# A trunk of gated DeltaNet and RWKV-7: more products behind the norms, the RWKV lora products first, convolution taps in PSUM

## The reference

```python
for i in range(2):
    h = h + 0.5 * rms_norm(swiglu(rms_norm(h, ng[0]), ffn_w_in, ffn_w_out), ng[1])
    u = rms_norm(h, ng[2])
    out = gdn_mixer(u, ...) if i == 0 else rwkv_mixer(u, ...)
    h = h + rms_norm(out, ng[3])
    h = h + 0.5 * rms_norm(swiglu(rms_norm(h, ng[4]), ...), ng[5])

def gdn_mixer(x, ...):
    qkv, z, b, a = split(x @ w_in)                  # 3072, 1024, 8, 8 columns
    qkv = silu(causal_dwconv(concat(conv_buf, qkv), conv_w))      # 4 taps
    q, k = l2_normalize(q), l2_normalize(k)         # per head
    o = rms_norm(chunk_gated_delta(q, k, v, g, beta, s0)) * silu(z)
    return o @ w_out

def rwkv_mixer(x, shift_prev, ...):
    x_prev = concat(shift_prev, x[:, :-1])
    xs = x[:, :, None] + (x_prev - x)[:, :, None] * lerp          # six mixes
    r, k, v = (xs[i] @ w_rkv[i] for i in 0, 1, 2)
    logw = f(w0 + tanh(xw @ w1) @ w2); a = sigmoid(a0 + (xa @ a1) @ a2)
    g = sigmoid(xg @ g1) @ g2
    kk = l2_normalize(heads(k * k_k))
    y = rwkv7_recurrence(r, decay, k, v, -kk, kk * a, s0)
    return (group_norm(y) + bonus) * g @ w_o
```

## Time and profile before

| | |
|---|---|
| median of 3 runs | 3081.12 us (3074.25 to 3081.9) |
| the profiled execution | 3077.95 us |
| its span, first to last instruction | 3076.2 us |
| mean granted TensorE clock | 0.934 of full speed |
| busy: PE, DVE, POOL, ACT | 2716.0, 1217.1, 1070.2, 859.6 us |
| instructions on PE, DVE, ACT, POOL | 26353, 1425, 1165, 506 |
| DMA | 202.15 MB, mean 66 GB/s |

### The profile page before, as it was taken

How to read it: one execution, slowest core, us unless ns; L and a number is a source line. 1 busy time by engine, 2 the same in 40 slices (tenths; PEclk the granted TensorE clock), 3 DMA queues, 4 the chain that set the end, 5 groups by cost and what they waited for, 6 DMA issues and landing times.

```text
span 3076.2 us, 60534 instructions
## 1 busy us (share of the span) xinstructions
PE 2716.0 (88%) x26353; PEld 2569.8 (84%) x26353; DVE 1217.1 (40%) x1425; ACT 859.6 (28%) x1165; POOL 1070.2 (35%) x506
## 2 busy tenths in 40 slices
PE   6999989977988799999899998677649888899997
PEld 6999989855874799999899997677438876899996
DVE  2333138815535443321433322332484455433312
ACT  3222232222321332222322222233413322422221
POOL 2444423323411334444244432232173321244432
PEclk9999999998986899999999998888759999999998
DMA  3223212210002222232122221121100011122321
GB/s 129 88 82 104 85 54 82 75 58 2 2 22 96 69 69 89 88 99 80 55 89 89 92 94 54 56 69 35 35 1 4 4 45 64 63 87 84 101 85 48
DMA packets 52570, 202.15 MB, mean 66 GB/s; under 512 B 6208, under 2 KB 6336, under 8 KB 52160
## 3 DMA queue, kind: packets, MB, share of 16 engines
q1 hardware_dynamic: 52416, 199.82, 19.4%
HBM read 190.12 MB, written 9.67 MB: 65 GB/s over the span
## 4 chain that ended last, share of the span: by engine, by line
PE 41%; issue 34%; POOL 11%; DVE 10%; ACT 1%; DMA 1%; DVEq 0%; POOLq 0%; SPq 0%; ACTq 0%
POOL wlo L271 10%; PE ps L301 10%; PE ps L299 10%; PE ps L300 10%; DVE cb L815 3%; PE ps L2022 1%; PE ps L2030 1%; PE ps L566 1%; PE ps L1973 1%; DVE sFM L2200 1%; PE ps L571 1%; PE ps L2081 1%; PE ps L1446 1%; DVE tb L1722 1%; PE ps L1978 1%
## 5 line engine op out<-in xcount | busy, mean ns | idle before, releaser
L271 POOL TENSOR_TENSOR wlo<-raw,whi 128x1024 fp32r<-128x1024 f32 (+1 forms) x316 | 834.5, 2643 | 1530.3 <-ACT whi L263 1530.3
L299 PE MATMUL ps<-xh,whi 128*128 128x272 f32 x3776 | 1107.7, 293 | 61.4 <-POOL wlo L271 40.5
L301 PE MATMUL ps<-xh,wlo 128*128 128x272 f32 x3776 | 1106.0, 293 | 0.0
L300 PE MATMUL ps<-xl,whi 128*128 128x272 f32 x3776 | 1098.9, 291 | 0.0
L299 PEld LDWEIGHTS ps<-xh,whi 128*128 128x128 f32 x3776 | 723.3, 192 | 77.5 <-POOL wlo L271 38.7
L300 PEld LDWEIGHTS ps<-xl,whi 128*128 128x128 f32 x3776 | 725.3, 192 | 0.0
L301 PEld LDWEIGHTS ps<-xh,wlo 128*128 128x128 f32 x3776 | 722.8, 191 | 0.0
L263 ACT ACTIVATE whi<-raw 128x1024 fp32r<-128x1024 f32 (+1 forms) x316 | 354.3, 1124 | 1277.6 <-PE ps L301 1230.6
L301 PE MATMUL ps<-mh,wlo 128*128 128x272 f32 x1408 | 406.3, 289 | 0.0
L300 PE MATMUL ps<-ml,whi 128*128 128x272 f32 x1408 | 405.5, 288 | 0.0
L299 PE MATMUL ps<-mh,whi 128*128 128x272 f32 x1408 | 405.2, 288 | 0.0
(11 more groups left out here) (397 smaller groups left out, 2919.0 us busy)
## 6 DMA issues: line engine op xcount, KB each, us to landing
raw<-w SPq DMA_DIRECT2D x252, 512.0 KB, 3.5
raw<-w SPq DMA_DIRECT2D x64, 704.0 KB, 4.0
h<-xT SPq DMA_DIRECT2D x1, 2176.0 KB, 11.1
yT<-h SPq DMA_DIRECT2D x1, 2176.0 KB, 6.6
Sst<-state_gdn SPq DMA_DIRECT2D x4, 512.0 KB, 3.5
SG<-state_gdn SPq DMA_DIRECT2D x4, 512.0 KB, 3.5
gdn_s_s<-gG SPq DMA_DIRECT2D x4, 512.0 KB, 2.6
gdn_s_s<-gT SPq DMA_DIRECT2D x4, 512.0 KB, 2.6
```

The source lines that it names most:

```text
L271: pool.tensor_tensor(wlo[two][:, 0:kt * P], raw[slot][:, 0:kt * P], whi[two][:, 0:kt * P].bitcast(F32), ALU.subtract).then_inc(w_lo, 1)
L299: pe.matmul(o, wh, hi[:, r, :], start=(start and k == 0), stop=False)
L300: pe.matmul(o, wh, lo[:, r, :], start=False, stop=False)
L301: mm = pe.matmul(o, wl, hi[:, r, :], start=False, stop=(stop and k == kt - 1))
```

## The change

- **Behind each pre-norm** (the four FFN inputs, the GDN input and now the lora units) PE runs units 0 and 1 and one half of unit 2 tile by tile, then unit 2's other half, the spread and unit 3. Units 0 and 1 have buffers of their own (`EARLY`), and units 0 to 2 are split during the last unit of the product before; unit 3 right behind the post-norm's root. A tiny square root in the same place (`warm`) loads ACT's table. The sums and spreads go to free columns of other banks. In post_norm_dve the low half of the tile before stands ahead of the update of h.
- **GDN input.** From unit 4 on the taps 0 to 2 accumulate in PSUM banks 4 to 7, and only two pairs of banks take units. ACT's split of unit 5 stands behind the second silu. The sums of squares follow one z unit later; the last pair comes after the b and a unit.
- **RWKV.** The lora products (w1|a1 and g1, each once plain and once scaled by the lerp, four units) go directly behind the norm, on the normed x; the token shift is applied to their results (lora_dve). Two rows of 24 matmuls with 8 columns take the carried shift state. DVE scales two raw units in place. The shift of x is done in two halves between the mixes of r; tanh, copy and sigmoid of the lora results stand on ACT between r and k; the squares and sums of k stand beside the units of v.

The core of the diff:

```diff
-    ("r", NM, NM), ("k", NM, NM), ("v", NM, NM), ("lora", 3, NM), ("wo", NM, NM),
+    ("lora", 4, NM), ("r", NM, NM), ("k", NM, NM), ("v", NM, NM), ("wo", NM, NM),
...
+        def early_hi(act, name, j):
+            n = BASE[name] + j
+            act.wait_ge(raw_in[n % 4], 16 * (n // 4 + 1))
+            if name == "lora" and j > 1:
+                act.wait_ge(R["lw_up"], past(R["lw_up"], j - 1))
+            free = 2 * (BASE[name] - (j < 3))
+            if free > 0:
+                act.wait_ge(acc, free)
+            dst = EARLY[name][0][j] if j < 2 else whi[n % 2]
+            act.activation(dst[:, 0:NM * P], raw[n % 4][:, 0:NM * P], ACT.Copy).then_inc(w_hi, 1)
...
+        def behind_norm_mm(pe, name, q):
+            behind_norm_tiles(pe, name, q)
+            behind_norm_half(pe, name)
+            spread_norm_pe(pe, q)
+            unit_mm(pe, name, 0, 3, pair(3), xh, xl)
+
+        def behind_norm_tiles(pe, name, q):
+
+            base = BASE[name]
+            bufs = [(EARLY[name][0][j], EARLY[name][1][j]) for j in range(2)] + [(whi[base % 2], wlo[base % 2])]
+            for k in range(NM):
+                pe.wait_ge(x_lo, 8 * SETS[name] + k + 1)
+                for j in range(3):
+                    if k == 0:
+                        pe.wait_ge(w_lo, base + j + 1)
+                    if j == 1:
+                        square_sum_pe(pe, q, k)
+                    first_products(pe, j, k, *bufs[j], halves=(0, 1) if j < 2 else (0,))
+            if q:
+                pe.wait_ge(h_upd, 8 * (q // 2))
+
+        def behind_norm_half(pe, name):
+            two = BASE[name] % 2
+            for k in range(NM):
+                first_products(pe, 2, k, whi[two], wlo[two], halves=(1,))
...
-                dve.tensor_tensor(tb[3][:, :, :], y[:, 2 * m:2 * m + 2, :], pair(3), ALU.mult).then_inc(h_tmp, 1)
+                dve.tensor_tensor(tb[3][:, :, :], y[:, 2 * m:2 * m + 2, :], post_rows(), ALU.mult).then_inc(h_tmp, 1)
+                if sett is not None and m:
+                    pre_norm_low(dve, q + 1, sett, m - 1)
                 dve.wait_ge(h_tmp, base + m + 1)
                 dve.scalar_tensor_tensor(h[:, 2 * m:2 * m + 2, :], tb[3][:, :, :], step,
                                          h[:, 2 * m:2 * m + 2, :], ALU.mult, ALU.add).then_inc(h_upd, 1)
-                if sett is not None and m:
-                    pre_norm_low(dve, q + 1, sett, m - 1)
...
                     if last and j >= 2:
                         split_hi(act, f"ffn{f}_out", 0, j - 2)
+                    elif first:
+                        if j == 0:
+                            split_hi(act, name, 0, 4)
+                            norm_copy_act(act, FFN_NORM[f])
+                        elif j == 3:
+                            split_hi(act, name, 0, 5)
                     else:
                         split_hi(act, name, 4 * i, j + 2)
...
+                    if last and j == 3:
+                        act.activation(warm[:, q // 2:q // 2 + 1], eps[:, 0:1], ACT.Sqrt)
+                        if then is not None:
+                            for jj in range(2 if then == "lora" else 3):
+                                early_hi(act, then, jj)
...
-                    split_hi(act, "gdn_in", 4 * i, j + 2)
                     if first and j == 0:
+                        split_hi(act, "gdn_in", 0, 4)
                         norm_copy_act(act, 2)
-                    else:
-                        silu_out(idx - 1, 1 - e)
+                        continue
+                    if not first:
+                        split_hi(act, "gdn_in", 4 * i, j + 2)
+                    elif j == 3:
+                        split_hi(act, "gdn_in", 0, 5)
+                    silu_out(idx - 1, 1 - e)
...
-                    n = EXT - 3
-                    dve.tensor_scalar(cb[e][:, 0:n], ext[e][:, 0:n], col(0), None, ALU.mult).then_inc(S["cv"], 1)
+                    part = two_rows(cb[e], 0) if first else taps_bank(e)
+                    dve.tensor_scalar(part, two_rows(ext[e], 0), col(0), None, ALU.mult).then_inc(S["cv"], 1)
                     for tap in range(1, 4):
                         dve.wait_ge(S["cv"], 5 * idx + 1 + tap)
-                        dve.scalar_tensor_tensor(cb[e][:, 0:n], ext[e][:, tap:tap + n], col(tap), cb[e][:, 0:n],
+                        dve.scalar_tensor_tensor(two_rows(cb[e], 0) if tap == 3 else part, two_rows(ext[e], tap), col(tap), part,
                                                  ALU.mult, ALU.add).then_inc(S["cv"], 1)
...
-            first_units_mm(pe, "gdn_in", q=2)
-            third_fourth_mm(pe, "gdn_in", 2)
-            with pe.Fori(1, NQKV // 4) as i:
+            behind_norm_mm(pe, "gdn_in", 2)
+            for j in range(4):
+                pe.wait_ge(S["ext_ready"], (1, 2, 5, 6)[j])
+                unit_mm(pe, "gdn_in", 4, j, pair(j % 2), xh, xl)
+            with pe.Fori(2, NQKV // 4) as i:
                 for j in range(4):
-                    pe.wait_ge(S["ext_ready"], 4 * i + j - 3)
-                    unit_mm(pe, "gdn_in", i * 4, j, pair(j), xh, xl)
+                    pe.wait_ge(S["ext_ready"], 4 * i + j - 1)
+                    unit_mm(pe, "gdn_in", i * 4, j, pair(j % 2), xh, xl)
 
             for m in range(HG):
-                if m < 3:
-                    pe.wait_ge(S["ext_ready"], NQKV - 3 + m)
+                if m < 2:
+                    pe.wait_ge(S["ext_ready"], NQKV - 1 + m)
+                elif m == 2:
+                    pe.wait_ge(S["cv"], 5 * (NQKV - 1))
                 else:
                     pe.wait_ge(S["z_scaled"], m - 2)
                 unit_mm(pe, "gdn_in", NQKV + m - m % 4, m % 4, pair(m % 3), xh, xl)
-                if m == 0:
-                    pe.wait_ge(S["ext_ready"], NQKV)
-                for t in (2 * m, 2 * m + 1):
-                    pe.wait_ge(S["l2_sq"], t + 1)
-                    sum_rows(pe, pair(3), one_col[:, 15 - t:31 - t], tb[t % 2], t == 0, t == 15).then_inc(S["l2_mm"], 1)
+                if m == 1:
+                    pe.wait_ge(S["cv"], 5 * NQKV)
+                if m > 0:
+                    l2_sums(pe, (2 * m - 2, 2 * m - 1))
...
+        def key_square_act(act, m):
+            if m == 0:
+                act.wait_ge(x_lo, 8 * SETS["wo"])
+            if m - 1 > 0:
+                act.wait_ge(R["kq_mm"], past(R["kq_mm"], m - 1))
+            act.activation(tb[m % 2][:, :, :], wh(k_, m), ACT.Square, scale=v(V_KK + m)).then_inc(R["kq_sq"], 1)
+
+        def key_sum_pe(pe, m):
+            pe.wait_ge(R["kq_sq"], past(R["kq_sq"], m + 1))
+            sum_rows(pe, pair(3), two_cols[:, 14 - 2 * m:30 - 2 * m], tb[m % 2], m == 0, m == NM - 1).then_inc(R["kq_mm"], 1)
...
+        def lora_scale_dve(dve):
+            for j, parts in ((2, ((3, slice(0, 64)), (4, slice(64, P)))), (3, ((5, slice(0, P)),))):
+                n = BASE["lora"] + j
+                dve.wait_ge(raw_in[n % 4], 16 * (n // 4 + 1))
+                w = raw[n % 4][:, 0:NM * P].rearrange("p (m c) -> p m c", c=P)
+                for i, c in parts:
+                    lerp = vec[:, V_LERP + i * NM:V_LERP + (i + 1) * NM].unsqueeze(2).broadcast_to([P, NM, c.stop - c.start])
+                    mul = dve.tensor_tensor(w[:, :, c], w[:, :, c], lerp, ALU.mult)
+                mul.then_inc(R["lw_up"], 1)
+            dve.wait_ge(R["sh_hi"], past(R["sh_hi"], 1))
+            dve.tensor_tensor(sh_l[:, :, :], shin[:, :, :], sh_h[:, :, :].bitcast(F32), ALU.subtract).then_inc(R["sh_lo"], 1)
...
+        def lora_out_act(act):
+            act.wait_ge(R["lora_up"], past(R["lora_up"], 12))
+            act.activation(lt1[0:64, :, :], LT[0][0:64, :, :], ACT.Tanh)
+            act.activation(lt1[64:P, :, :], LT[0][64:P, :, :], ACT.Copy).then_inc(R["lora_cp"], 1)
+            act.activation(lg[:, :, :], LT[1][:, :, :], ACT.Sigmoid).then_inc(R["lora_cp"], 1)
+            act.wait_ge(R["lora_cp"], past(R["lora_cp"], 2))
...
+            base = BASE["lora"]
+
+            def carried(j):
+                n = base + j
+                pe.wait_ge(w_lo, n + 1)
+                o = ps[:, 6, HALF + NB * (j - 2):HALF + NB * (j - 1)]
+                for k in range(NM):
+                    wh_, wl_ = (t[n % 2][:, k * P:(k + 1) * P] for t in (whi, wlo))
+                    pe.matmul(o, wh_, sh_h[:, k, :], start=(k == 0), stop=False)
+                    pe.matmul(o, wh_, sh_l[:, k, :], start=False, stop=False)
+                    pe.matmul(o, wl_, sh_h[:, k, :], start=False, stop=(k == NM - 1))
+            behind_norm_tiles(pe, "lora", 8)
+            pe.wait_ge(R["sh_lo"], past(R["sh_lo"], 1))
+            carried(2)
+            behind_norm_half(pe, "lora")
+            carried(3)
+            pe.wait_ge(R["lora_raw"], past(R["lora_raw"], 2))
+            spread_norm_pe(pe, 8)
+            unit_mm(pe, "lora", 0, 3, pair(3), xh, xl)
...
+                dve.tensor_tensor(prev[:, :, :], prev[:, :, :], rs[:, :, :], ALU.mult).then_inc(up, 1)
```

(18 more changed lines are left out.)

274 lines of the change are left out of this document (158 added, 116 removed).

## The result

The kernel after takes 2985.32 us (median of four runs, 2982.70 to 2988.54); the kernel before, beside it, 3078.62 (four runs). The ratio is 0.9698, with a 95% interval of 0.9680 to 0.9716: 93.3 us less. The forecast was 2986.

A forecast was written before the change was run, and what follows sets the result against it. TensorE (PE), busy for 88% of the span, was taken as the bound, with gains where it stands idle. Terms sum to -94.5 against 3077.95: 2983.5, forecast 2986 since the median is 3.2 above that execution; range 2960 to 3014.

The forecast's parts named there:

- The three sites: Norms in front of the three inner FFN inputs: -4.8, -5.1 and -4.7 us, bounds -2 and -7 each.
- the start: Kernel's start, up to the first FFN's end: only the product's part of the norm gain, -2.5 us (0 to -3).
- just over DVE's pace of about 2.25: Tiles behind the norms: 15 matmuls and sums take 2.4 us at full clock, just over DVE's 2.25.
- The reciprocal behind `sh_l`: RWKV head: reciprocal behind DVE's wait for ACT's copy of the shift state, some 2.4 us before the first lora product.
- 4.8 for 2 x 24 tiny matmuls ... between them: RWKV head, before r: 48 tiny matmuls at 0.1 us each, taken between bounds of nothing and 7.9.
- r itself: RWKV: the shift's second half between the mixes of r adds 4 us (0 to +8).
- r to k: RWKV: ACT's tanh, copy and sigmoid with two table loads ahead of the next weights add 4.4 us.
- v's eight sums: RWKV, in v: eight sums of 1.0 us, of which about 5 us show.
- The first rival: Convolution: DVE stays the bound, as PSUM-writing instructions are held up or take longer; 2999 us, chance 0.13.
- the second: RWKV gives back half, its new head being one long chain through DVE and ACT; +20, 3006 us, chance 0.15.
- the third: Convolution: DVE's PSUM accumulation makes the kernel slower than before, from about 2.4 us per instruction; 3097 at 2.6, chance 0.02.
- the fourth: Norm parts do little, longer tiles running at the low clock; -1 at three sites and start, 2999 us, chance 0.10.

The follow-up runs named there:

- The late splits: Kernel after, but units 0 to 3 behind each of five norms are all split behind the post-norm's root: 3004.56 us, 0.9757.
- the other trace: The kernel after run once more, unchanged, on one chip with three edits: 2987.09 us, 0.9708; span 2979.6. Also called the second trace.
- the old RWKV stage's run: Kernel after, but the RWKV mixer up to the norm of k as before, lora last on mixed x: 3029.49 us, 0.9836.
- the sums of k's norm: Kernel after, but squares of k beside k's units and all eight sums in PE's gap between k and v: 2976.84 us, 0.9677.

## Why the prediction held, step by step

**Norms: right in size, wrong in one reason.** The three sites gave -5.8, -4.8 and -4.7 for -4.8, -5.1 and -4.7; the start -2.4 for -2.5. The late splits show that the early ones are worth 3.8 a norm, through POOL's absence beside `h` and `xl`. The step "just over DVE's pace of about 2.25" failed: PE is the bound of the tiles, before (2.08 us each) as after (2.45), and no worth of the half unit abreast is seen (2986.03 without it). The last norm gave 0.1 for 0.4.

**Convolution: right.** Forecast: four instructions of about 0.85, a DVE unit near 5.2, PE the bound at 6.04. Measured: 0.81, and PE units 6.04 apart. The first z unit ends 13.1 us earlier (13.2 forecast): at 600.5, one unit before the first sums at 606.51, and 172.0 us behind the first FFN instead of 185.1. The timeline of after: the first DVE unit with taps in PSUM, from one unit's first scaling (L875) to the next, and the copy of a later unit beside POOL's split:

```profile
484.62 0.43 DVE L875 TENSOR_TENSOR ext<-ps,rs 128x272 f32<-128x272 f32 x1
...
489.62 0.17 DVE L894 COPY cnew<-ext 128x3 f32 x1
489.77 0.44 DVE L875 TENSOR_TENSOR ext<-ps,rs 128x272 f32<-128x272 f32 x1
...
578.86 1.12 DVE L894 COPY cnew<-ext 128x3 f32 x1
...
577.56 2.40 POOL L300 TENSOR_TENSOR wlo<-raw,whi 128x1024 fp32r<-128x1024 f32 x1 [3.65 <-ACT whi L275]
```

That unit takes 5.15 us (489.77 - 484.62). Later each takes 6.04, because the copy of three columns is held until POOL's split ends (577.56 + 2.40 = 579.96; the copy ends at 579.98). This wait costs nothing: POOL is paced by ACT, ACT by PE, and the slack of 0.9 is DVE's to lose. In before POOL's split stood beside the three multiply-adds and cost 2.24.

The Trainium skill (VectorE: DVE Perf Modes, section "Why PSUM operands drop a tier") says that an operand in PSUM caps fp32 at the slowest mode. The multiply agrees: 516 ns for 568 columns into SBUF, 812 into PSUM. By that alone the change adds 0.3 a unit; the lock it escapes was worth more.

**z part: right.** Forecast -23 between the first z unit and the spread; it takes 69.7 us (670.14 - 600.5) instead of 92.7, and the whole GDN input gave -36.1 for -36. The sums in their own unit cost 14.6, by the trace in PE's wait for ACT's squares (15.5).

**RWKV: right in sum, with four terms off.** From FFN2's last product to r's first it is 58.4 us (57.0 in the other trace), 54.6 forecast. Two terms failed. The reciprocal behind `sh_l` cost 3.3, priced at 2.4. And "4.8 for 2 x 24 tiny matmuls ... between them" was right for themselves (5.3) but left out the clock that they lose in this trace: half unit 2 took 4.60 at 0.63 where 3.0 was forecast, and the spread and unit 3 8.7 where 7.1 was. In the second trace these took 3.1 and 7.2. r itself took 3.9 more for 4, and r to k was 4.7 longer for 4.4: right. PE at the end of v in after:

```profile
2101.32 4.17 PE L627 MATMUL ps<-tb,mf 128*16 128x272 f32 x16
2106.50 2.18 PE L1981 MATMUL ps<-lt,wa 64*128 64x272 f32 x16 [1.02 <-ACT tb L2003]
...
2118.04 2.10 PE L1794 MATMUL ps<-tb,halves 128*128 128x272 f32 x8 [1.39 <-ACT RB L2007]
```

Here the sums are mis-sized in the other direction: v's eight sums all show (four of 1.09 inside v, four in the 4.17 behind it), +8.5 for +5; from the last of them to the norm of k it is 12.5 us (2118.04 - 2105.49), where 17 was forecast and 24.6 stood: -12.1 for -7.7. Of the 3.3 priced for the root and two table loads PE waited only 1.02 us, since the root's load ran beside the last sums and the sigmoid's beside the first decay products. The terms' errors, up to 4.4 each way, partly cancel: -38.3 for -41 in these traces; by its medians the old stage costs 44.2.

**The rest.** Sum of the terms: -94.5 forecast, -89.7 between the two spans, -93.3 between the medians. That the median hits 2986 to within 1 us is luck: the terms of RWKV alone were off by more, and four executions of one kernel lie 5.8 apart. The first rival (DVE stays the bound) is refuted by the one wait for DVE that is left in after, the second by the old RWKV stage's run, the third by the 0.81 us, the fourth by the late splits' 3.8 a norm. The 3.3 us more behind the norm of k are no effect of the change: that stretch takes 422.6 to 432.4 us in traces with the same code. Why it varies so is open. Two small slips stand in the prediction's sums: 3.2 + 1.3 + 0.45 + 0.3 for a norm with a table load is 5.25, not 5.1, and 2983.5 + 3.2 is 2986.7.

## What to carry to other kernels

Look for the place where a DVE instruction meets a POOL instruction of known time, and count its operands in SBUF: a scratch tile in PSUM takes it out of the way, and work split a product earlier takes POOL out of the way. Sums that depend on another engine belong one unit later, or better into a gap that PE waits in anyway, as the sums of k's norm showed (10 us of their stage, in one trace). Price very narrow products by more than their own time: the 48 matmuls of 8 columns cost that and, in nine traces of eleven, the clock of what followed.

## What the runs showed of the hardware

- The granted clock fell to 0.63 behind 24 back-to-back matmuls of 8 columns, with PE busy for all of 2.60 and 4.60 us. It fell there in nine traces of eleven, and stayed at 1.00 in two and in the one run without them. I had expected it to fall only behind idle time.
- A DVE copy of 128x3 took 1.12 us in place of 0.16 when it met a POOL subtract, and ended with it. The Trainium skill (SBUF — State Buffer, section "SBUF: two separate sides") gives the lock to DVE instructions in a two-port mode as well as to those with two SBUF inputs; the copy, with one input, fits the first kind, though no run shows its mode. I had looked at the multiply-adds alone, though before has such a copy too: 2.36 us at 480.72, beside a subtract from 480.15 to 483.06.
- A DVE multiply-add of 568 columns takes 0.81 us whether it writes PSUM or SBUF, with one operand in PSUM, while POOL's 2.40 runs beside it.
